# MoE units of a hybrid decoder layer on one core: the sums of the unit before, in front of the gate and up product instead of behind it

## The reference, cut to what matters

```python
scores = sigmoid(x @ w_router)               # 64 experts, the best 8 are kept per token
h = silu(x @ w_gate[e]) * (x @ w_up[e])      # (tokens, 256), 1024 -> 256
h = h * gate[:, e]
y += h @ w_down[e]                           # 256 -> 1024
y += (silu(x @ ws_gate) * (x @ ws_up)) @ ws_down   # the shared expert
```

## Time and profile before

| what | value |
|---|---|
| time before, median of 3 runs | 1015.59 us (1015.31 to 1017.05) |
| the profiled execution: its own time | 1017.33 us |
| its span | 1015.5 us |
| PE busy, share of the span | 931.5 us, 92% |
| VectorE / ScalarE / GpSimd busy | 49% / 23% / 24% |
| read from HBM over the span | 263.75 MB |

### The profile page before, as it was taken

The page is one execution under the profiler, slowest core; times in us unless marked ns, Lnnn a source line. Parts: engine busy times, 40 slices in busy tenths (PEclk is TensorE's granted clock), DMA queues, the critical chain, the costliest instruction groups (busy, mean ns, idle before and its releaser), DMA issues.

```text
span 1015.5 us, 19351 instructions
## 1 busy us (share of the span) xinstructions
PE 931.5 (92%) x7882; PEld 564.9 (56%) x7882; DVE 500.6 (49%) x1040; ACT 232.7 (23%) x483; POOL 243.5 (24%) x281
## 2 busy tenths in 40 slices
PE   4999999999999997779999999999999799899895
PEld 4878877887787777536834344443343234333332
DVE  2148857885787486985623333432323233323225
ACT  3231134113411351254112111111111111111213
POOL 0039904960794099100100000000000000000000
PEclk9999999999999999979999999999999899999989
DMA  8633144214412408139589999999999999999961
GB/s 243 184 125 95 31 125 142 65 44 138 126 55 84 139 2 290 27 140 419 199 361 406 395 419 420 419 420 419 419 420 420 418 415 419 420 414 419 419 282 44
DMA packets 76741, 265.04 MB, mean 261 GB/s; under 512 B 12942, under 2 KB 44240, under 8 KB 51799
## 3 DMA queue, kind: packets, MB, share of 16 engines
q1 hardware_dynamic: 72791, 254.09, 64.5%
q0 software_dynamic: 3856, 9.64, 2.5%
HBM read 263.75 MB, written 5.89 MB: 266 GB/s over the span
## 4 chain that ended last, share of the span: by engine, by line
PE 62%; DMA 23%; DVE 6%; SPq 3%; ACT 3%; issue 2%; DVEq 0%; ACTq 0%
PE bank L1333 60%; DMA big<-in_w_up 22%; SPq L401 2%; ACT big L1630 2%; DMA big<-in_w_in 1%; PE bank L628 1%; DVE big L1920 1%; ACT L1630 1%; DVE big L1977 1%; DVE big L1973 0%; DVE big L897 0%; DVE big L1168 0%; SPq L1228 0%; PE bank L693 0%; DVE big L1983 0%
## 5 line engine op out<-in xcount | busy, mean ns | idle before, releaser
L1333 PE MATMUL bank<-big 64*64 64x64 f32 (+8 forms) x7412 | 872.1, 373 | 61.5 <-DMA big<-in_w_up 27.6
L1333 PEld LDWEIGHTS bank<-big 64*64 64x64 f32 (+4 forms) x7412 | 509.1, 143 | 406.8 <-issue 336.3
L1630 ACT ACTIVATE big<-bank 128x512 f32<-128x512 f32 (+8 forms) x283 | 121.7, 459 | 620.2 <-PE bank L1333 473.7
L1174 POOL DMA_INDIRECT big<-xg,big x26 | 25.9, 995 | 506.4 <-PE bank L628 399.6
L2119 POOL TENSOR_SCALAR big<-big 128x256 f32<-128x256 f32 x120 | 127.0, 1059 | 0.4
L1045 DVE TENSOR_TENSOR big<-big,bank 128x256 f32<-128x256 f32 x26 | 11.0, 422 | 210.3 <-ACT big L1630 210.3
L2131 POOL TENSOR_TENSOR big<-big 128x256 f32<-128x256 f32 x120 | 87.4, 729 | 0.3
L1083 DVE TENSOR_TENSOR big<-big,bank 128x512 f32<-128x512 f32 x104 | 71.5, 688 | 12.7 <-PE bank L1333 11.3
L1920 DVE SCALAR_TENSOR_TENSOR big<-big 128x256 f32<-128x256 f32 x120 | 74.0, 617 | 4.1
L990 DVE TENSOR_SCALAR big<-bank 128x1 uint32<-128x1 f32 x26 | 4.1, 156 | 112.8 <-PE bank L1333 112.5
L1630 ACT ACTIVATE big<-big 128x272 f32<-128x272 f32 (+9 forms) x108 | 49.8, 505 | 42.6 <-DVE big L1855 11.3
(11 more groups left out here) (156 smaller groups left out, 356.8 us busy)
## 6 DMA issues: line engine op xcount, KB each, us to landing
big<-in_w_gate SPq DMA_DIRECT2D x64, 1024.0 KB, 17.9
big<-in_w_up SPq DMA_DIRECT2D x64, 1024.0 KB, 23.6
big<-in_w_down SPq DMA_DIRECT2D x64, 1024.0 KB, 25.2
big<-in_w_in SPq DMA_DIRECT2D x29, 1024.0 KB, 5.4
big<-in_w_out SPq DMA_DIRECT2D x2, 2048.0 KB, 12.1
big<-in_state_wkv SPq DMA_DIRECT2D x32, 64.0 KB, 2.2
out_wkv_s<-big SPq DMA_DIRECT2D x32, 64.0 KB, 3.9
big<-in_x_prompt SPq DMA_DIRECT2D x2, 512.0 KB, 3.2
```

Of the source, the lines that this page charges most:

```text
L1174: pool.indirect_dma_start(out=x[0:n, :], out_offset=None, in_=xg, in_offset=bass.IndirectOffsetOnAxis(ap=idxu[0:n, col:col + 1], axis=0), ...
L1333: return nc.tensor.matmul(out_, lhsT=lhsT, rhs=rhs, start=start, stop=stop)
L1630: return nc.scalar.activation(out_, in_, f, **kw)
```

## The change

Three orders are rewritten, and two waits adapted.

- PE turns the gates first and does the sums of the preceding unit before `gate_up(q)`; after `gate_up(q)` comes `turn(q + 1)`, then `turn_hidden(q)` and at once `down(q)`.
- ScalarE copies the turned tokens of the next unit before the turned hidden values.
- VectorE does `gates`, `fetch_rows` and `take_gates` at the start of a pair, then the shared rows, `add_late`, `onehot`, and `hidden(q)` last.
- `turn_gates(q)` waits for the first sum of unit q - 2 (before: q - 1), since the combine of q - 1 now comes behind it. `combine(q)` waits for the copied gates of unit q + 1 too, since they lie in the columns of bank 0 that it writes.

```diff
@@ -686,7 +686,7 @@
 
                 pe.wait_ge(S['og_ready'], q + 1)
                 wait(pe, 'g_ready', q)
-                wait(pe, 'cb_sum', NC * (q - 1) + 1 if q >= 1 else 0)
+                wait(pe, 'cb_sum', NC * (q - 2) + 1 if q >= 2 else 0)
                 pe.wait_ge(S['idx_ready'], min(q + 4, NU_E))
                 for t in range(3):
                     r = tile_rows(t)
@@ -695,7 +695,7 @@
 
             def combine(q):
 
-                pe.wait_ge(S['g_ready'], q + 1)
+                pe.wait_ge(S['g_ready'], min(q + 2, NU_E))
                 pe.wait_ge(S['idx_ready'], min(q + 5, NU_E))
                 pe.wait_ge(S['ye_act'], 2 * q + 2)
                 pe.wait_ge(S['xet_ready'], 2 * min(q + 2, NU_E))
@@ -718,13 +718,13 @@
                     count = pe.value_load(cnti[0:1, 0:1])
                 if DOWN_AT <= q < DOWN_AT + NDOWN:
                     shared_down(q - DOWN_AT)
-                gate_up(q)
+                turn_gates(q)
                 if q:
                     combine(q - 1)
-                turn_hidden(q)
-                turn_gates(q)
+                gate_up(q)
                 if q + 1 < NU_E:
                     turn(q + 1)
+                turn_hidden(q)
                 down(q)
 
             with pe.If(count > SLOTS):
@@ -838,9 +838,9 @@
                     act.wait_ge(S['cnt_ready'], 1)
                     count = act.value_load(cnti[0:1, 0:1])
                 sigma(q)
-                hidden_turned(q)
                 if q + 1 < NU_E:
                     turned(q + 1)
+                hidden_turned(q)
                 store(q)
             with act.If(count > SLOTS):
                 for c in range(1, MAXPASS):
@@ -1046,17 +1046,17 @@
                 note(v.tensor_tensor(hid[q % 2], hid[q % 2], ps_gu[q % 2][:, FE:2 * FE], M), 'hid_ready')
 
             def pair(q):
+                gates(q)
                 if q + 3 < NU_E:
                     fetch_rows(q + 3)
+                take_gates(q)
+                if DOWN_AT <= q < DOWN_AT + NDOWN:
+                    shared_rows(q - DOWN_AT)
+                if q:
+                    add_late(q - 1)
                 if q + 4 < NU_E:
                     onehot(q + 4)
-                gates(q)
-                if DOWN_AT <= q < DOWN_AT + NDOWN:
-                    shared_rows(q - DOWN_AT)
                 hidden(q)
-                if q:
-                    add_late(q - 1)
-                take_gates(q)
 
             def gates(q):
                 wait(dve, 'g_mm', q)
```

## The result

The changed kernel takes 1041.69 us (median of 4 runs, 1040.66 to 1045.63) against 1016.32 us before: 1.0253 times the time, 95% interval 1.0236 to 1.0271. That is 25.4 us slower, in the stated range (1018 to 1044), but nearly twice the +14 that was forecast, and above the 1023 to 1040 of the case that the forecast took as the likely one.

What follows compares the result with a forecast made beforehand. Transfers bound the kernel before, with PE's pace close by; the change was to make PE the slower. Stops +7.4 and transfers +6, near-equal, taken as +8, plus clock +6, gave +14: 1029.6 us, range 1018 to 1044, likeliest case 1023 to 1040.

Steps and rivals of the forecast that it cites:

- the two paces: PE's work, 34.5 to 36.4 us per P and T unit together, against transfers' 40.0; PE forecast to become the slower.
- The four covers: Four places where work no longer covers a latency; new stops of 49.9 us in all, replacing 43.0 us of standing.
- (a): At turn_gates, waiting until VectorE has read the index from bank 0: some 0.35 us in 13 units, 4.55 in all.
- (b): In front of combine(q - 1), waiting for unit q's gates out of bank 0: 0.6 us in each unit.
- (d): Between turn_hidden and down, waiting for the copied turned hidden values, now covered by nothing: 0.75 us per unit.
- (c): Hidden chain from gate_up to turn_hidden, now covered only by turn(q + 1): 0.4 us per unit, 1.0 more in unit 25.
- the 437.1 us of work: PE's work from turn_hidden of unit 0 to unit 25: 16 units of 17.26, 9 of 18.18, less 0.9 for three.
- The clock: PE clock falls at heads of units without shared piece: bounds 0 and 13 at 1.7 us; four taken, 6.8, counted +6.
- The transfers' own end: Late loads lose 8 to 10 us until about unit 4; last w_up near 993.5, end at 1006.7: +6.
- The stops hide: Rival: new stops fall where PE stood anyway, transfers set the end; +1 to +7, 1017 to 1023; chance 0.17.
- The clock falls in most units: Rival: falls at unit heads and between gate_up and down, some 19 at 1.7 us; 1047 (1040 to 1055); chance 0.13.
- Faster: Rival: combine done while PE waits, 8.5 instead of 11.1 us behind last weights; 2.6 to 2.8 us earlier, 1012.8; chance 0.06.

Runs made afterwards that it cites:

- experiment 2: Changed kernel with index(q + 3) moved from the head of the unit to behind turn_hidden(q), fetch_rows behind hidden(q): 1023.27 us, 1.0067 of the kernel before.
- experiment 3: Changed kernel with the sample product last of the five in each combine, so only it waits for the copied gates: 1024.97 us, 1.0085 of the kernel before.
- experiment 4: Changed kernel with the index behind turn_hidden and the sample product last in each combine: 1022.89 us, 1.0053 of the kernel before.
- Experiment 9: Changed kernel plus an unread 384-column product behind turn_gates in units 1 to 25: 1037.87 us, 1.0208 of the kernel before.
- experiment 7: Order before in units 0 to 9, the changed order without edits from unit 10 on: 1020.17 us, 1.0029 of the kernel before.
- experiment 5: Order before in units 0 to 9; from unit 10 changed order with index behind turn_hidden and sample product last in combine: 1013.80 us, 0.9981 of the kernel before.
- experiments 1: Changed order in units 24 and 25 alone, the order before in units 0 to 23: 1016.72 us, 0.9993 of the kernel before.

## Why the prediction came out as it did

**Which of the two paces sets the time: right.** With the changed order PE no longer stands for weights in any unit (the list of waits after), and its own sum closes to 0.1 us (next paragraph). Experiments 2 to 4 give the stops back one by one, and the wait for w_up returns with each: 7.8, 7.1, 15.2 us.

**The four covers: right in place, a tenth short in size.** 49.9 us were forecast, 54.7 measured. By units, start to start: (a) 0.41 instead of 0.35 in 13 units; (b) 0.63 instead of 0.6; (d) 0.75 as forecast; (c) 0.55 instead of 0.4. That is 25 x 1.93 + 13 x 0.41 = 53.6. The last three units add 0.53, 0.36 and 0.36, since the combine there also waits longer for the store than the forecast 0.2: 54.8 in all. The forecast's 1.0 for unit 25 did not come. It was counted twice: the stop there is longer because no `turn` covers it, but the 437.1 us of work hold 25 turns, and in the changed kernel only 24 lie between the two points. Unit 25 takes 18.65 us like unit 24 (1001.36 to 1020.01 and 982.71 to 1001.36). The term that was mis-sized is (c), 25 times 0.15 us: it was made from the profile's idle time of 1.40 us, which begins at the modelled end of the last matmul, while what stood in front of the stop ended, for the purpose of issuing, 0.16 us earlier. Two experiments show them apart: experiment 3 took away (b) alone (19.59 to 18.97 us per P unit), experiment 2 (a) and (d) (19.59 to 18.75, 1.16 less the 0.3 that came back in front of the combine).

**The clock: right in kind, four falls forecast, seven found.** 6.8 us forecast (6 in the sum), 11.6 measured. This is the step that was furthest off, and it was a choice between bounds of 0 and 13. All seven begin where a unit without a shared piece begins: behind 0.9 us of one-column matmuls and the stops (a) and (b). Of the nine units that have `shared_down` there, none has one. Experiment 9 puts work in place of (b) and leaves all else, and in its trace the falls in the units are gone; experiment 3 takes (b) away, and they are gone too. Experiment 2 keeps (b) but has neither the index nor (a) in front of it, and no unit from 1 on has one at its head. So it takes both: the one-column matmuls with (a), and (b) behind them. The mean clock over the span says the same of all executions: 0.976 to 0.980 in the four of the changed kernel, 0.989 to 0.991 in the four of experiment 3, 0.985 to 0.988 in those of experiment 2; only experiment 9 is divided.

Which of the 13 places gets a fall is another matter. Here all seven P units have one and none of the six T units, but the kind of unit does not decide: in experiment 7, with the same order, the falls lie in the P units 15 and 17 and the T units 18, 20 and 22. That it came to seven, and not to four or to thirteen, is in part chance, and what picks the units stays open. An edit also shifts the times at which the units begin; that a mere shift spared all 13 places in three kernels is unlikely, but was not tried apart. The rule of the Trainium skill ("TensorE: Matmul & The Clock Gate", HAM oscillation), that long waits for transfers are what brings the clock down, would have given 0: here no stop was longer than 1.0 us from unit 1 to 24, and the measurement decides against it as the only cause.

**The transfers' own end: nearly right, and not what set it.** 8 to 10 us of loss in the first units were forecast for a PE with few stops; experiment 4, the nearest to that, has 7.2. In the changed kernel itself the transfers lost 13.0 us between 520 and 580 us, since PE's stops delay them too. The forecast of +6 from this side would have held only as a floor, and the time was set by PE alone.

**Where the other 11 us are.** The forecast let PE end the last `down` at 1008.0 us, and added 6 us for the clock and 0.6 for two paces near each other. It ended at 1024.7 us: 4.8 us more of stops, 11.6 us of falls and 0.2 us of a later start. That is 10 us above the forecast in the trace, and 11.4 by the medians. Stops and clock both cost more than forecast, and nothing made up for it. The range held because its upper end was made from a fall at each of the 13 places; that the time lies inside it says little for the four falls of the forecast.

**The rivals.** "The stops hide": no, 54.7 us against 43.0. "The clock falls in most units": its time, 1040 to 1055, holds the measured one, but its mechanism did not come: 7 of 25, and none in the second place, between `gate_up` and `down`, until the last `down` of five of the experiments, where there is no `turn` over the first stop. (Its 1047 does not follow from its own terms either: +8 and 19 falls at 1.7 us make 1056.) "Faster": its mechanism exists, 8.5 instead of 11.1 us behind the last landing (experiment 5), but only where PE still waits for weights at the last unit.

**Where the 25 us lie by units.** Experiment 7 says it most plainly. In the first ten units PE was the slower of the two before the change as well, each us added there lengthens the time, and some 22 of the 25 us come from them. Later the transfers need 20.0 us per unit anyway, and the changed order's 19.6, or 20.4 with a fall in each second unit, only just exceeds it.

## What to carry to other kernels

Before work is moved in an order written by hand, write beside each instruction what latency it covers where it stands; moving a 4 us product uncovers at both ends, and the stops of both ends are paid in each round in which that engine is the slower. Read that latency where it is bare (a first or last unit), from start to start and not from the idle count. Where an engine's pace and that of the transfers lie within a few per cent, one order need not fit all rounds: the old order while the ring is full and the new one where the engine waits gave 0.2%, the only gain that these runs found.

## What the runs showed of the hardware that was not expected

Short stops brought TensorE's clock down. A stop of 0.4 and one of 0.6 us with three transposes between, behind 0.9 us of one-column matmuls, were followed by 3.4 us at 1.2 GHz in seven units, each 1.65 us of work longer; a 1.4 us stop and a 0.5 us stop around two transposes did the same in the last `down` of experiments 1, 3, 4, 7 and 9, and not in that of experiments 2 and 5, nor in that of the changed kernel. A product that nobody reads, in the place of one 0.6 us stop, kept the clock up in the traced execution and cost less there than the falls (5.3 us against 11.6).

The index lies in bank 0 in columns of its own, and `turn_gates` waits until VectorE has read it all the same. The Trainium skill ("PSUM — Partial Sum Buffer", bank collisions) says why: two engines must not access one bank at a time in the same partitions. No run here tried it; what the traces show is the price of obeying it, (a) above, 0.41 us in 13 units. (b) is another case: the sample sums are written into the columns in which the gates lie, so they would have to wait even without that rule, and another order of the same five products avoids the stop.
